# Delta rule preparation: the deferred projection matmuls of a tile in one gap at its end in place of three gaps inside it

## The chip, the cores and the metric

One Trainium2 chip (trn2), one of its cores. The metric is the device time of one execution in microseconds (us); each kernel's time is the median of its runs. Engines are named as in the profile: PE is TensorE (PEld its weight loads), DVE VectorE, ACT ScalarE, POOL GpSimd, SP SyncE, which here only issues DMAs.

## What is computed

The reference is a network of three layers in float32: an attention and gated-scan layer, a second gated-scan layer, and a layer that mixes pooling, a state-space scan and a gated delta rule, followed by experts. Only the delta rule's preparation matters here. For each chunk of 64 tokens and each of 6 heads (in both directions of time) it needs, of the normalised q and k:

```python
gc = jnp.cumsum(to_chunks(g), axis=-1)
decay = jnp.exp(jnp.where(lower, gc[..., :, None] - gc[..., None, :], -jnp.inf))
kb = kc * bc[..., None]
xm = jnp.where(strict, jnp.einsum('bnhik,bnhjk->bnhij', kb, kc) * decay, 0.0)
attn = jnp.einsum('bnhik,bnhjk->bnhij', qc, kc) * decay
```

Independent of it, the same layer needs the projection of the layer's input `hT` (1024 channels by 1024 tokens) onto 896 channels `xbcT`, which a later stage (a convolution) reads. The kernel computes this projection beside the delta rule's preparation.

## The kernel before, in words

The kernel is a sequence of stages; each is a function that writes the instruction stream of every engine by hand, with semaphores between them, and ends with a barrier of all engines. The stage here is `gdn_prepare` (line 2719). Its tile loop runs over ten tiles of 128 tokens (two chunks) in the order 8, 9, 0, 7, 1, 6, 2, 5, 3, 4 (`TILE_ORDER`); tiles 8 and 9 are context and have no attention product. The loop stands once in each engine's block, with `k` the place in the order. `GH` is 6 heads, in `PAIRS` = 3 pairs.

- PE (lines 2814 to 2841): `decays(k, 1)`, six matmuls of 128 columns into the two banks `ps_r`; transposes of q and k into `ps_t` (line 2824); `decays(k, 0)`, six matmuls into the same two banks (line 2808), which first waits for `arg_done`, that DVE has read the banks; the kk products (line 2832) and from the third tile on the kq products (line 2839).
- DVE (lines 2896 to 2903): `args(k, 1)` reads `ps_r` into `dec` (line 2875); `attend(k - 1)` (lines 2888, 2892); `norm(k + 2)` (line 2862); `args(k, 0)` (line 2877), which reads `ps_r` again.
- ACT (lines 2914 to 2928): moves q and k transposed to SBUF (line 2918), the kk products (line 2925), and takes the exponential of `dec` (line 2928) once `args(k, 0)` is done.
- POOL (lines 2790 to 2796): `H` = kk x decay (line 2793), then `attend(k - 1)` (line 2788).
- SP (lines 2755 to 2766): per tile four small DMAs of `H`'s diagonal blocks (line 2761) and, for the eight tiles with attention, two DMAs of 384 KB (line 2766).

The projection is the class `Background` (line 243). Its work is cut into units (7 here, of 128 channels, with one weight load of 512 KB each) and fills (14 here, two of 512 tokens per unit). A fill is 8 matmuls of 512 columns into one of two PSUM banks (line 342; in float32 each shows as two records), one move of the bank by ACT into one of three stage buffers (line 359) and one store of 256 KB by SP (line 304). The first `LEAD` = 3 fills run ahead of the loop. The matmuls of the others, 88, are dealt out evenly over the `slots` that the constructor is told:

```python
g = f if f < lead else lead + min(slots - 1, spent * slots // total)
```

A slot may hold parts of two fills. `multiply(pe, g)` (line 329) issues the matmuls of slot `g`; `move(act, g)` (line 351) moves the banks whose fill ended in slot `g - 1`; `transfer(sp, g)` (line 314) stores the fills that ended in slot `g - 2`, and loads the weights of the unit three further once a unit ended in slot `g - 1`. Ahead of a new fill PE waits for its bank's last move; ahead of a move ACT waits for the landing of the store that used its stage buffer before. Before the change a tile has three slots: behind `decays(k, 1)`, behind `decays(k, 0)`, and at the end of the tile (lines 2817, 2827, 2841). The next stage, `gdn_base`, begins with memsets on POOL (line 2977).

Of the kernel before, what the change touches and what calls it, by code (L numbers as in the profile page):

```python
# [21 lines left out]
def wait(eng, sem, value):  # L22

    if not isinstance(value, int) or value > 0:
        eng.wait_ge(sem, value)


def own_semaphores(nc, ctx, tag):

    used = []  # L30

    def clear():
        nc.clear_and_free_semaphores(used)
        nc.all_engine_barrier()

    def make(name):
        used.append(nc.alloc_semaphore(name=f"{tag}_{name}"))
        return used[-1]

    ctx.callback(clear)  # L40
    return make
# [2185 lines left out]
T2 = ROWS2 // P  # L2227
# [487 lines left out]
def unit_of(t, d):  # L2715
    return next(2 * s + d for s in range(STEPS) if order(s, d) == t)


def gdn_prepare(nc, tag, tok, beta, cum, logs, k_n, qT, kT, H, beta_rows, diag, attn_out, jobs):

    LEAD = 3
    with ExitStack() as ctx:
        sb = lambda n, s, d=F32: ctx.enter_context(nc.sbuf_tensor(f"{tag}_{n}", s, d))
        sem = own_semaphores(nc, ctx, tag)
        pbank = lambda n: ctx.enter_context(nc.psum_tensor(f"{tag}_{n}", [P, BANK], F32))
# [14 lines left out]
         arg_done, kk_moved, exp_done, kq_done, h_done, beta_turned, beta_moved, beta_stored, diag_stored) = (sem(n) for n in names)  # L2740
        att_done = [sem(f"att_done{d}") for d in range(2)]
        att_stored = [[sem(f"att_stored{d}{b}") for b in range(2)] for d in range(2)]
        bg = Background(sb, sem, pbank, jobs, 3 * T2, 3, 2, 3, lead=LEAD)
        block = ctx.enter_context(nc.Block())

        @block.sync
        def _(sp):
            for n, dst in ((1, k_n), (0, q_n)):
                sp.dma_start(dst[:, :, :], tok[:, n * GW:(n + 1) * GW].rearrange("(t p) c -> p t c", p=P)).then_inc(loaded, 16)
            bg.begin(sp)  # L2750
            sp.wait_ge(beta_moved, 1)
            sp.dma_start(beta_rows, beta_T[0:2 * T2 * GH, :]).then_inc(beta_stored, 16)
            for g in range(LEAD):
                bg.transfer(sp, g)
            for k, t in enumerate(TILE_ORDER):
                for n in range(3):
                    bg.transfer(sp, LEAD + 3 * k + n)
                b, at = k // HALF, k % HALF * GH
                sp.wait_ge(h_done, k + 1)
                for q in range(QUARTERS):  # L2760
                    sp.dma_start(diag[b, q, at:at + GH, :].rearrange("h (j i) -> j h i", i=SUB),
                                 H[SUB * q:SUB * (q + 1), t, :, SUB * q:SUB * (q + 1)]).then_inc(diag_stored, 16)
                if t < TILES:
                    for d in range(2):
                        sp.wait_ge(att_done[d], k - CTX_STEPS + 1)
                        sp.dma_start(attn_out[unit_of(t, d)], att[d][:, k % 2, :, :].rearrange("p h i -> p (h i)")).then_inc(att_stored[d][k % 2], 16)
            bg.end(sp)
            sp.wait_ge(beta_stored, 16)
            sp.wait_ge(diag_stored, 16 * QUARTERS * T2)
            for d in range(2):  # L2770
                for b in range(2):
                    sp.wait_ge(att_stored[d][b], 16 * TILES // 2)
# [25 lines left out]
        @block.tensor  # L2798
        def _(pe):
            pe.wait_ge(consts, 1)  # L2800
            pe.transpose(ps_t[0][0:2 * T2 * GH, 0:P], nbeta[:, :, :, :].rearrange("p k h d -> p (k h d)"), ident[:, :]).then_inc(beta_turned, 1)

            def decays(k, d):
                t = TILE_ORDER[k]
                wait(pe, arg_done, 2 * k + 1 - d)
                for h in range(GH):
                    col = 2 * SH + d * GH + h
                    last = pe.matmul(ps_r[h // 3][:, (h % 3) * P:(h % 3 + 1) * P], logs[:, t, col:col + 1].to_broadcast([P, P]),
                                     mask[:, d, :], start=True, stop=True)
                last.then_inc(r_made, 1)  # L2810

            for g in range(LEAD):
                bg.multiply(pe, g)
            for k, t in enumerate(TILE_ORDER):
                cols = slice(t * P, (t + 1) * P)
                decays(k, 1)
                bg.multiply(pe, LEAD + 3 * k)
                pe.wait_ge(normed, 2 * k + 2)
                if k == 0:
                    pe.wait_ge(beta_moved, 1)  # L2820
                for m, src in enumerate((q_n, k_n)):
                    wait(pe, kk_moved, 2 * k + m - 1)
                    for g in range(PAIRS):
                        last = pe.transpose(ps_t[m][:, g * P:(g + 1) * P], src[:, t, g * P:(g + 1) * P], ident[:, :])
                    last.then_inc(turned, 1)
                decays(k, 0)
                bg.multiply(pe, LEAD + 3 * k + 1)
                pe.wait_ge(t_moved, 2 * k + 2)
                for h in range(GH):
                    part = slice(GE * (h % 2), GE * (h % 2) + GE)  # L2830
                    out = slice(h // 2 * P, (h // 2 + 1) * P)
                    last = pe.matmul(ps_t[h % 2][:, out], kT[part, h // 2, cols], kT[part, h // 2, cols], start=True, stop=True)
                last.then_inc(kk_made, 1)
                if k >= CTX_STEPS:
                    wait(pe, kq_done, k - CTX_STEPS)
                    for h in range(GH):
                        part = slice(GE * (h % 2), GE * (h % 2) + GE)
                        out = slice(h // 2 * P, (h // 2 + 1) * P)
                        last = pe.matmul(ps_kq[h % 2][:, out], kT[part, h // 2, cols], qT[part, h // 2, cols], start=True, stop=True)
                    last.then_inc(kq_made, 1)  # L2840
                bg.multiply(pe, LEAD + 3 * k + 2)

        @block.vector
        def _(dve):
# [60 lines left out]
        @block.scalar  # L2905
        def _(act):
            act.wait_ge(beta_turned, 1)
            act.activation(beta_T[0:2 * T2 * GH, :], ps_t[0][0:2 * T2 * GH, 0:P], ACT.Copy).then_inc(beta_moved, 1)
            act.wait_ge(squared, 2 * T2)
            act.wait_ge(consts, 1)  # L2910
            act.activation(std[:, :, :], norms[:, :, :], ACT.Sqrt, bias=eps[:, 0:1]).then_inc(std_done, 1)
            for g in range(LEAD):
                bg.move(act, g)
            for k, t in enumerate(TILE_ORDER):
                bg.move(act, LEAD + 3 * k)
                for m, dst in enumerate((qT, kT)):
                    act.wait_ge(turned, 2 * k + m + 1)
                    act.activation(dst[:, :, t * P:(t + 1) * P], ps_t[m][:, 0:PAIRS * P].rearrange("p (g i) -> p g i", g=PAIRS),
                                   ACT.Copy).then_inc(t_moved, 1)
                bg.move(act, LEAD + 3 * k + 1)  # L2920
                act.wait_ge(kk_made, k + 1)
                wait(act, h_done, k - 1)
                for m in range(2):
                    out = kk[:, k % 2, :, :].rearrange("p (g m) i -> p m g i", m=2)[:, m]
                    act.activation(out, ps_t[m][:, 0:PAIRS * P].rearrange("p (g i) -> p g i", g=PAIRS), ACT.Copy).then_inc(kk_moved, 1)
                bg.move(act, LEAD + 3 * k + 2)
                act.wait_ge(arg_done, 2 * k + 2)
                act.activation(dec[:, k % 2, :, :], dec[:, k % 2, :, :], ACT.Exp).then_inc(exp_done, 1)
            bg.move(act, LEAD + 3 * T2)


def gdn_base(nc, tag, beta_rows, diag, lower_rows, upper_rows, jobs):
# [1228 lines left out]
```

## Time and profile before

| | us |
|---|---|
| median of 3 runs | 4562.99 |
| lowest, highest | 4560.31, 4571.77 |
| profiled execution, its own time | 4572.53 |
| span of the profiled execution, first to last instruction | 4570.8 |
| mean granted TensorE clock (share of full speed) | 0.902 |

The profile is of one execution. The page gives shares of the whole span; the stage of the change takes some 180 us of it, so it is read from the table of stretches (busy time of each engine between two times), the list of waits and the timeline, each for that stretch. Times in the timeline are from the span's start. Durations of matmuls are modelled and overlap the next one's; the distance from one start to the next is what PE takes.

### The profile page before, as it was taken

The numbers are of one execution on the slowest core, as the hardware profiler recorded it, in microseconds if no ns is written. First come the engines' busy times: TensorE is split into PE (matmuls) and PEld (weight loads), VectorE is DVE, ScalarE is ACT, GpSimd is POOL, SyncE is SP. The second block draws the span as 40 slices with busy tenths as digits, with TensorE's granted clock in tenths as the row PEclk, the third lists the DMA queues.
The fourth block names the chain that finished last, engine by engine and source line by source line (L and its number), as shares of the span: only waits on it lengthen the run. The fifth ranks groups of instructions, "written<-read, shape, count | busy, mean of one in ns | idle before, by whom it ended". The sixth has DMA issues, their size and how long they took to land. (4 is left out here: it accounts for less than half of the span.)

```text
span 4570.8 us, 48008 instructions
## 1 busy us (share of the span) xinstructions
PE 3763.4 (82%) x17093; PEld 2428.5 (53%) x17093; DVE 1523.2 (33%) x3680; ACT 1077.4 (24%) x2188; POOL 1013.3 (22%) x911
## 2 busy tenths in 40 slices
PE   7899998997989999999997938967755836765996
PEld 3545776763445666665684425654445835332442
DVE  1012223321532433535431220054476547142001
ACT  0023333321322333323323420021112101110111
POOL 0000002321331333333432440001302534110110
PEclk9999998998999999999998967988877858877998
DMA  3243213247421111111114321362334520444996
GB/s 103 75 124 92 80 40 106 86 147 244 153 97 38 45 50 54 38 47 41 56 43 190 124 101 56 91 165 84 108 83 124 175 92 24 172 165 144 318 318 225
DMA packets 423952, 516.34 MB, mean 113 GB/s; under 512 B 71954, under 2 KB 327482, under 8 KB 423731
## 3 DMA queue, kind: packets, MB, share of 16 engines
q1 hardware_dynamic: 390131, 473.04, 31.3%
q10 hardware_dynamic: 28992, 23.65, 1.6%
q0 software_dynamic: 4608, 16.78, 1.4%
q8 instruction: 130, 2.13, 0.2%
q14 instruction: 91, 0.75, 0.1%
HBM read 378.70 MB, written 134.68 MB: 112 GB/s over the span
## 5 line engine op out<-in xcount | busy, mean ns | idle before, releaser
L622 PE MATMUL hgrn_ps_w<-xT,hgrn_ring 128*128 128x512 f32 x1152 | 507.6, 596 | 0.0
L594 POOL TENSOR_TENSOR hgrn_queries<-hgrn_qd,hgrn_pair_decay 128x640 f32<-128x640 f32 x192 | 285.6, 1506 | 415.0 <-PE hgrn_ps_a L673 198.5
L622 PEld LDWEIGHTS hgrn_ps_w<-xT,hgrn_ring 128*128 128x128 f32 x1152 | 217.0, 192 | 251.7 <-issue 251.6
L1139 PE MATMUL end_ps_z<-end_w,end_yT 128*128 128x512 f32 x768 | 338.1, 600 | 4.4 <-ACT end_yT L1088 2.4
L618 PE MATMUL hgrn_ps_w<-hgrn_ring,xT 128*128 128x256 f32 x1536 | 337.8, 379 | 0.0
L618 PEld LDWEIGHTS hgrn_ps_w<-hgrn_ring,xT 128*128 128x128 f32 x1536 | 289.0, 190 | 38.2 <-issue 0.5
L1139 PEld LDWEIGHTS end_ps_z<-end_w,end_yT 128*128 128x128 f32 x768 | 146.6, 193 | 185.7 <-issue 178.7
L774 DVE COPY_PREDICATED hgrn_scores<-hgrn_mask,hgrn_ps_s 128x128 f32<-128x128 uint32 x192 | 48.5, 297 | 469.0 <-issue 466.7
L346 PE MATMUL gla_bg_ps<-gla_bg_w,xT 128*128 128x256 f32 x768 | 187.6, 397 | 4.6 <-DMA gla_bg_w<-in_w_in_ab_dram 4.6
L346 PEld LDWEIGHTS gla_bg_ps<-gla_bg_w,xT 128*128 128x128 f32 x768 | 150.6, 200 | 38.0 <-issue 10.8
L872 ACT ACTIVATE hgrn_k_tok<-hgrn_ps_a 128x256 f32<-128x256 f32 x84 | 32.3, 384 | 548.8 <-PE hgrn_ps_a L648 548.8
L240 DVE COPY in_stage<-in_ps 128x512 f32<-128x512 f32 (+4 forms) x29 | 17.8, 615 | 394.8 <-PE in_ps L184 303.2
L342 PE MATMUL att_bg_ps<-xT,att_bg_w 128*128 128x512 f32 (+1 forms) x288 | 135.5, 610 | 13.1 <-POOL att_ident L1442 13.1
L184 PE MATMUL in_ps<-hT_cols,in_wbuf 128*128 128x512 f32 x288 | 126.6, 603 | 0.0
L1516 DVE COPY att_stage<-att_ps_o 128x128 f32<-128x128 f32 x96 | 28.0, 292 | 291.7 <-PE att_ps_o L1478 291.7
L1703 POOL TENSOR_TENSOR gla_queries<-gla_qd,gla_pair_decay 128x640 f32<-128x640 f32 x64 | 84.2, 1334 | 184.3 <-PE gla_ps_o L1766 130.6
L1537 ACT ACTIVATE att_p_sb<-att_s_sb,att_shift 128x256 f32<-128x256 f32 (+1 forms) x192 | 88.8, 464 | 146.9 <-DVE att_shift L1512 146.9
L184 PE MATMUL in_ps<-xT,in_wbuf 128*128 128x512 f32 x256 | 112.6, 603 | 13.0 <-DMA in_wbuf<-in_w_in_ab_dram 13.0
L3990 PE MATMUL exp_ps_d<-expw_wd,exp_hidT 128*128 128x512 f32 x256 | 114.1, 599 | 11.0 <-ACT exp_hidT L3937 11.0
L346 PE MATMUL att_bg_ps<-att_bg_w,xT 128*128 128x256 f32 x512 | 122.5, 385 | 0.0
L342 PE MATMUL gdnp_bg_ps<-hT,gdnp_bg_w 128*128 128x512 f32 x224 | 106.5, 617 | 18.4 <-DMA gdnp_bg_w<-in_w_in_dram 9.5
L579 POOL TENSOR_TENSOR hgrn_kd<-hgrn_key,hgrn_rel 128x1024 f32<-128x1024 f32 x24 | 59.9, 2497 | 277.3 <-ACT hgrn_rel L861 277.1
(575 smaller groups left out, 6743.6 us busy)
## 6 DMA issues: line engine op xcount, KB each, us to landing
expw_wg<-in_exp_w_gate_dram SPq DMA_DIRECT2D x16, 2048.0 KB, 10.6
expw_wu<-in_exp_w_up_dram SPq DMA_DIRECT2D x16, 2048.0 KB, 16.2
expw_wd<-in_exp_w_down_dram SPq DMA_DIRECT2D x16, 2048.0 KB, 21.8
gla_bg_w<-in_ada_w_dram SPq DMA_DIRECT2D x24, 1024.0 KB, 5.3
hgrn_ring<-in_w_in_c_dram SPq DMA_DIRECT2D x36, 512.0 KB, 4.0
end_gt<-gate_l SPq DMA_DIRECT2D x16, 768.0 KB, 7.2
hgrn_ring<-in_w_in_c_dram SPq DMA_DIRECT2D x12, 1024.0 KB, 5.4
hgrn_o<-hgrn_o_stage SPq DMA_DIRECT2D x192, 64.0 KB, 2.6
```

The lines of the kernel that those rows point to most:

```text
L184: last = pe.matmul(bank[0:job.rows, 0:job.span], w[:, k, b * job.rows:(b + 1) * job.rows], job.acts[:, k, s:s + job.span], start=(k == 0), ...
L342: last = pe.matmul(bank[0:job.rows, 0:job.span], w[:, k, b * job.rows:(b + 1) * job.rows], job.acts[:, k, s:s + job.span], start=(k == 0), ...
L346: last = pe.matmul(bank[0:job.rows, q * job.width:(q + 1) * job.width], job.acts[:, k, t * P:t * P + job.rows], w[:, k, 0:job.width], star ...
L579: pool.tensor_tensor(kd[:, b, d, :], key[:, d, :], rel[:, d, :], ALU.mult).then_inc(k_done, 1)
L594: pool.tensor_tensor(queries[:, d, s, :].rearrange("p (b a c) -> p b a c", b=POINTS, a=PC), q, f, ALU.mult).then_inc(queries_done, 1)
L618: last = pe.matmul(bank[:, q * 2 * P:(q + 1) * 2 * P], xT[:, k, t * P:(t + 1) * P], wt[:, k, :], start=(k == 0), stop=(k == KB - 1))
L622: last = pe.matmul(bank[:, :], wt[:, k, 0:P], xT[:, k, part * BANK:(part + 1) * BANK], start=(k == 0), stop=(k == KB - 1))
L774: dve.copy_predicated(scores[:, d, p % 2, :], mask[:, d, :].bitcast(U32), ps_s[g % 2][:, d * P:(d + 1) * P]).then_inc(scores_done, 1)
L1139: made = pe.matmul(ps_z[h][:, :], yT[:, k, :], w[:, k, h * BANK:(h + 1) * BANK], start=(k == 0), stop=(k == NB - 1))
L1537: last = act.activation(p_sb[:, s % 2, h, 0:wide(d)], s_sb[:, s % 2, h, 0:wide(d)], ACT.Exp, bias=shift[:, s % 2, h:h + 1], scale=0.125, a ...
L1703: pool.tensor_tensor(queries[:, d, s, :].rearrange("p (b a c) -> p b a c", b=POINTS, a=PC), q, f, ALU.mult).then_inc(queries_done, 1)
L3990: last = pe.matmul(ps_d[g][:, :], hidT[:, j, :], wd[:, b, j, g * BANK:(g + 1) * BANK], start=(j == 0), stop=(j == FB - 1))
```

## The change

The constructor is told `T2` = 10 slots where it was told 30. On PE the calls of `multiply` behind the two decay groups go, and the one at the end of the tile stays. On ACT the moves ahead of kk and ahead of the exponential go, and the one at the top of the tile stays. On SP one `transfer` per tile stays of three. `LEAD`, the rings, banks and stage buffers stay as they are.

```diff
-        bg = Background(sb, sem, pbank, jobs, 3 * T2, 3, 2, 3, lead=LEAD)
+        bg = Background(sb, sem, pbank, jobs, T2, 3, 2, 3, lead=LEAD)
...
             for k, t in enumerate(TILE_ORDER):
-                for n in range(3):
-                    bg.transfer(sp, LEAD + 3 * k + n)
+                bg.transfer(sp, LEAD + k)
...
                 decays(k, 1)
-                bg.multiply(pe, LEAD + 3 * k)
                 pe.wait_ge(normed, 2 * k + 2)
...
                 decays(k, 0)
-                bg.multiply(pe, LEAD + 3 * k + 1)
                 pe.wait_ge(t_moved, 2 * k + 2)
...
-                bg.multiply(pe, LEAD + 3 * k + 2)
+                bg.multiply(pe, LEAD + k)
...
             for k, t in enumerate(TILE_ORDER):
-                bg.move(act, LEAD + 3 * k)
+                bg.move(act, LEAD + k)
...
-                bg.move(act, LEAD + 3 * k + 1)
                 act.wait_ge(kk_made, k + 1)
...
-                bg.move(act, LEAD + 3 * k + 2)
                 act.wait_ge(arg_done, 2 * k + 2)
...
-            bg.move(act, LEAD + 3 * T2)
+            bg.move(act, LEAD + T2)
```

## Rows read from the trace of the kernel before

**Rows 1.** The page: busy time of the engines, us (share of span) and instructions

```profile
PE 3763.4 (82%) x17093; PEld 2428.5 (53%) x17093; DVE 1523.2 (33%) x3680; ACT 1077.4 (24%) x2188; POOL 1013.3 (22%) x911
```

**Rows 2.** Stretch: its us, busy us (count) PE PEld DVE ACT POOL, clock, DMA share, GB/s

```profile
3145.50:3258.50 113.00, 113.00 (x623) 70.66 (x622) 48.39 (x142) 28.66 (x56) 24.82 (x14) 1.00 0.26 81
```

**Rows 3.** Waits from 3143 to 3275 us: total us, times, longest

```profile
DVE gdnp_dec L2875 <- PE gdnp_ps_r L2808: 64.2, 10, 7.6
```

**Rows 4.** Timeline of a steady tile (k = 5): start us, us, engine, line

```profile
3207.34 1.50 PE L2808 MATMUL gdnp_ps_r<-gdnp_mask,logs 128*128 128x128 f32 x12
...
3208.67 2.74 PE L342 MATMUL gdnp_bg_ps<-hT,gdnp_bg_w 128*128 128x512 f32 x6
...
3208.94 1.64 DVE L2875 TENSOR_SCALAR gdnp_dec<-gdnp_ps_r,cum 128x128 f32<-128x128 f32 x6 [5.64 <-PE gdnp_ps_r L2808]
...
3210.50 1.01 DVE L2888 TENSOR_TENSOR gdnp_kq<-gdnp_ps_kq,gdnp_dec 128x384 f32<-128x384 f32 x2
...
3211.25 0.49 PE L2824 MATMUL gdnp_ps_t<-gdnp_ident,gdnp_q_n 128*128 128x128 f32 x3
...
3211.91 1.50 PE L2808 MATMUL gdnp_ps_r<-gdnp_mask,logs 128*128 128x128 f32 x12
3212.16 0.48 ACT L2918 ACTIVATE gdn_kT<-gdnp_ps_t 128x384 f32<-128x384 f32 x1
...
3213.24 2.74 PE L342 MATMUL gdnp_bg_ps<-hT,gdnp_bg_w 128*128 128x512 f32 x6
...
3213.59 1.65 DVE L2877 SCALAR_TENSOR_TENSOR gdnp_dec<-gdnp_ps_r,cum,gdnp_dec 128x128 f32<-128x128 f32 x6
...
3215.92 0.94 PE L2832 MATMUL gdnp_ps_t<-gdn_kT 64*128 64x128 f32 x12
...
3216.90 0.87 ACT L2925 ACTIVATE gdnp_kk<-gdnp_ps_t 128x384 f32<-128x384 f32 x2 [4.25 <-PE gdnp_ps_t L2832]
...
3217.45 2.84 PE L342 MATMUL gdnp_bg_ps<-hT,gdnp_bg_w 128*128 128x512 f32 x6
3217.66 0.60 ACT L359 ACTIVATE gdnp_bg_stage<-gdnp_bg_ps 128x512 f32<-128x512 f32 x1
...
3218.14 0.85 ACT L2928 ACTIVATE gdnp_dec<-gdnp_dec 128x768 f32<-128x768 f32 x1
...
3220.13 1.50 PE L2808 MATMUL gdnp_ps_r<-gdnp_mask,logs 128*128 128x128 f32 x12
```

**Rows 5.** Timeline of the second scan stage: PE starts on a release by DVE

```profile
1470.94 0.49 DVE L763 TENSOR_TENSOR hgrn_k_end<-hgrn_kd,hgrn_end_decay 128x128 f32<-128x128 f32 x2
1471.49 0.20 PEld L648 LDWEIGHTS hgrn_ps_a<-hgrn_ident,hgrn_k_end 128*128 128x128 f32 x2 [0.57 <-DVE hgrn_k_end L763]
```

**Rows 6.** Timeline of the stage's tail, from the last tile's first decay group

```profile
3258.53 1.50 PE L2808 MATMUL gdnp_ps_r<-gdnp_mask,logs 128*128 128x128 f32 x12
...
3263.78 10.64 SPq L2766 DMA_DIRECT2D gdn_attn<-gdnp_att  x2
...
3268.85 0.84 ACT L2928 ACTIVATE gdnp_dec<-gdnp_dec 128x768 f32<-128x768 f32 x1
...
3271.54 4.28 POOL L2788 TENSOR_TENSOR gdnp_att<-gdnp_kq,gdnp_mask 128x768 f32<-128x768 f32 x2
...
3274.95 2.17 SPq L2761 DMA_DIRECT2D gdnp_diag<-gdn_H  x4
...
3278.12 0.47 SPq L304 DMA_DIRECT2D xbcT<-gdnp_bg_stage  x1
3282.35 0.21 POOL L2977 MEMSET gdnb_rows<- 128x128 f32 x1 [6.53 <-POOLq L34]
```

**Rows 7.** DMA issues from 3140 to 3300 us: count, KB each, us to landing

```profile
xbcT<-gdnp_bg_stage SPq DMA_DIRECT2D x12, 256.0 KB, 2.8
```

**Rows 8.** Stretches behind an idle time of PE, and with short ones (columns as rows 2)

```profile
3137.00:3141.00 4.00, 4.00 (x6) 1.79 (x7) 2.42 (x6) 0.29 (x1) 0.00 (x0) 0.59 0.76 191
...
950.00:960.00 10.00, 6.67 (x47) 5.57 (x46) 7.56 (x15) 1.47 (x3) 3.72 (x2) 1.00 0.33 116
```

## The prediction, made before the changed kernel was run

> **What bounds the kernel now.** I read the page first: TensorE (PE) is busy for 82% of the span, no other engine for more than 53% even with PE's own weight loads counted [rows 1]. The page's chain of waits is followed back only a short way, through the last stage, and says nothing of this one, so I went to that stage, `gdn_prepare`, with the table of stretches: its tile loop runs from 3145.5 us, and tiles 0 to 8 fill 113.0 us in which PE is busy all 113.0 and the granted clock is 1.00, the upper of its two levels, 2.4 GHz [rows 2]. The list of waits in the loop has DVE, ACT and POOL waiting for PE or for each other, the largest for PE being DVE's 64.2 us on the first decay group [rows 3], and no wait of PE. The loop is bound by PE's own instructions.
>
> The timeline of one steady tile (k = 5) is what the working rests on [rows 4]. PE's starts give the pitch of each part: first decay group 3207.34 to 3208.67, 1.33 us; three deferred matmuls (each shows as two records) to 3211.25, 2.58; six transposes to 3211.91, 0.66; second decay group to 3213.24, 1.33; three deferred to 3215.92, 2.68; kk and kq, twelve records each, to 3217.45, 1.53, so about 0.77 each; three deferred to 3220.13, 2.68. Sum 12.79 us, with nothing between. One deferred matmul costs 0.86 (2.58/3); the other two gaps are 0.10 longer, and I take that for the switch to the narrower matmuls behind them.
>
> **The change, part by part.** The 88 deferred matmuls behind the lead were spread over 30 gaps of three (two of them have two: the third of tile 4 and the very last); by the same rule of `Background` they now fall into 10 gaps of 9, 9, 9, 9, 8, 9, 9, 9, 9, 8. Nothing is computed more or less.
>
> (a) PE's work. The nine deferred matmuls of a tile cost the same in one place. Two of three switches to wide matmuls and back go. The one at the transposes shows no price, the one at the next tile's decay group stays, and the one at kk saves between 0 and 0.10, according to whether kk behind other 128-column matmuls costs the same bubble. I take 0.07 off.
>
> (b) The gap between the decay groups was cover. The second group, `decays(k, 0)`, overwrites the two banks that DVE is still reading for the first, so it waits for `arg_done`. DVE begins 1.60 us after the first group's start (3208.94) and needs six instructions, 1.64 us [rows 4], so it is done at 3.24. Today PE comes to that wait at 3211.91 - 3207.34 = 4.57 and never stops. Without the gap it comes at 1.33 + 0.66 = 1.99. How soon PE starts after DVE is shown by the scan stage: DVE ends at 1470.94 + 0.49 = 1471.43, PE's weight load starts at 1471.49 [rows 5], 0.06 later; I add 0.05 for a weight load that no running matmul hides. The group starts at 3.35: **a new stall of 1.36 us per tile**, in all ten. Bounds: 1.25 (no wake-up) and 1.42 (0.06, and a whole pitch of a decay record, 1.33/12 = 0.11, unhidden).
>
> (c) The gap before kk covered ACT's moves of qT and kT. It is not missed: the transposes are out at about 2.2, ACT's two moves of 0.48 end near 3.0, and the second decay group ends only at 3.35 + 1.33 = 4.68. kq needs DVE's first half of attend(k-1): 3.24 + 1.01 = 4.3, against kq's start at 5.5 [rows 4]. Cost nothing; if this cover went, kk would wait for ACT.
>
> (d) The other chain. DVE's second arguments start where they do now, since DVE has attend and norm in between: 3213.59 - 3207.34 = 6.25, end 7.9. But today ACT's Exp starts only at 3218.14, 10.8 into the tile, because kk and a bank's move stand ahead of it. Now kk ends near 5.7, ACT's copies (0.87) near 6.6, Exp runs 7.9 to 8.8, and POOL's `H` and attend(k-1), 2.1 each by the pair in [rows 6], end by 13. This is off PE's path, PE being at its nine deferred matmuls from 6.3 to 14.0. Nothing in it becomes later.
>
> (e) Moves, stores and loads. At the top of a tile ACT moves at most what the last gap filled, 0.60 us each [rows 4], before the transposes are out at 2; once, in tile 9, two banks, the second held until fill 9's store has landed (issued near 12.9 of tile 8, 2.8 later landed), so ending near 2.2 and then delaying qT by 0.3, still ahead of 4.68. SP's stores come two gaps after the fill, which is now two tiles in place of two thirds of one; three stage buffers just carry that. Weight loads are issued from tiles 1, 3 and 5 for use in 4, 6 and 8: tens of us ahead. Cost nothing inside the loop.
>
> Tile length: 12.79 + 1.36 - 0.07 = 14.08, that is +1.29 (1.25 - 0.10 = 1.15 to 1.42). The last tile starts nine tiles in: **+11.6 us** (10.4 to 12.8).
>
> (f) The tail. From the last tile's start, 3258.53, Exp ends at 3269.69, 11.16 in; POOL runs H and the two last attends; SP is behind it: it is held by tile 8's att (issue ends at 3263.78 + 10.64 = 3274.42), then issues a store, four diag (2.17), two att (about 1.0, from 3277.1 to 3278.12) and the last store (0.47) to 3278.59, and with 2.8 us to landing the stage ends near 3281.4, 22.9 in [rows 6, 7]. In the changed tile Exp ends at about 7.85, 3.3 earlier. The chain behind it moves with it: SP's last att issue ends at 16.25. Against that, fills 11 and 12 are now stored there too, two issues more, 2 x 0.48; last issue at 17.7, landing 20.5. PE's last eight matmuls, 6.9 us from 6.3, end at 13.2 and the last bank moves by 16.2 even if it waits for the store of fill 10 to land; that is hidden behind SP. Three stores and two att close together share the queues: I give back 0.4. So **-2.0 us**, between -3.3 (Exp's whole lead) and +1.9 (lead worth nothing, 0.96 of issues and as much again of traffic).
>
> Sum: 11.6 - 2.0 = **+9.6 us**. Against the profiled execution's own 4572.53 (span 4570.8) that is 4582.1; that execution lies 9.5 us above the median of the three runs, 4562.99, and nothing in it is particular to this stage, so I put the sum on the median: **4572.6 us**, +0.21%. What a measurement of this kernel can tell from no change is about 0.3%, 13.7 us, so this counts as no change.
>
> **Rivals.** *The clock falls.* Waits come back into a loop that had none. After PE's long idle time before the third lead bank the clock is 0.59 over four us, 4 x 0.41 = 1.64 us of full-speed work lost [rows 8]; in each of nine tiles that is +14.8, in all +24.4, 4587 us, slower. It decides as soon as three tiles in nine do it (9.6 + 3 x 1.64 = 14.5). Against it: a stretch of ten us in another stage has PE busy for 6.67 us only and still a granted clock of 1.00 [rows 8], and here PE would be busy for 12.7 in 14.1. The Trainium skill (TensorE: Matmul & The Clock Gate, "A second HAM failure mode: psum-queue depth-cycling") tells of a kernel whose short idle times between groups of matmuls made the clock go back and forth; by that rule each of the ten waits could cost a slow start. The trace so far does not agree. Chance 0.05.
>
> *The tail takes instead of giving.* The mechanism is the ring of three stage buffers: the last bank may be moved only when fill 10's store has landed, and this store stands on SP behind POOL's attend(8); then three stores follow the att pair. At +1.9 in place of -2.0, with a stall of 1.42, the sum is 12.8 + 1.9 = +14.7, 4577.7, slower. It decides if the tail gives nothing back and a tile grows by 1.5. For it: SP is the last engine at work already [rows 6]. Against: Exp's lead of 3.3 us is plain arithmetic. With the scatter of the runs (11 us over three) that can push a true +9.6 over the line: 0.20.
>
> *Faster.* That needs the removed switches to be worth more than the stall: rows allow 0.10 a tile at the most against 1.25, unless the tail or the scatter gives it. To end at -13.7 some 23 us would have to come from nowhere. That the change does not do what it says (PE would not stop at the second group, since DVE had finished there) is ruled out by the order of the code unless DVE's work is shorter than its record. Both together 0.05.
>
> **The numbers.** Forecast 0.70. Its own range is 10.4 - 3.3 = +7.1 to 12.8 + 1.9 = +14.7, and 3 to 4 us on either side for the scatter of medians: 4566 to 4581. This holds the forecast and the tail rival; the clock's 4587 is left out. Faster 0.05, same 0.70, slower 0.25.
>
> **What would show it.** In the changed profile: starts of the first decay group 14.0 to 14.1 us apart; a wait of PE at the second decay group on DVE's first arguments, ten times, 1.2 to 1.4 us; no wait of PE at kk; granted clock 1.00 throughout the loop; Exp near 8 us into the tile; from the last tile's start to the next stage's first POOL memset about 22 us where it is 23.8 now [rows 6]. I would be wrong if the tile grew by more than 1.5, if PE waited at kk for ACT, or if a clock below 1.00 stood in the loop.

## The result, and the profile after

The changed kernel took 4577.34 us (median of 8 runs, 4570.51 to 4590.55), the kernel before 4570.01 (median of 8, 4560.31 to 4574.23; the three runs shown above are among them). The ratio is 1.0021 with a 95% interval of 1.0012 to 1.0031, which is +9.6 us (5.5 to 14.2) on 4570: a small loss, inside the 0.3% that the prediction called no change, but clear of zero. (The two medians differ by 7.3 us, which lies in the same interval.)

The profiled execution of the changed kernel has a span of 4574.6 us, only 3.8 more than the one before; it reached the first tile 5.9 us sooner (3139.60 against 3145.54), so the two are compared stage by stage and not by their spans. Line numbers of the stage have moved up by one to five (the decay groups are now L2807, the first arguments L2872). The page first:

```profile
PE 3760.2 (82%) x17093; PEld 2425.0 (53%) x17093; DVE 1519.9 (33%) x3680; ACT 1078.9 (24%) x2188; POOL 1011.6 (22%) x911
```

The same 17093 matmul records, the same shares [rows 1]: nothing of the change is to be seen here. The stretch of tiles 0 to 8, in the table of stretches (length, then busy time and count of PE, PEld, DVE, ACT and POOL, then clock, DMA share and GB/s):

```profile
3139.60:3265.20 125.60, 115.27 (x623) 72.73 (x622) 48.39 (x142) 30.29 (x56) 26.84 (x15) 1.00 0.24 74
```

It had been 113.0 us with PE busy throughout [rows 2]; now it is 125.6, with the same 623 PE records, DVE's busy time to the hundredth what it was, and some 10 us in which PE does nothing. The granted clock is still 1.00. The list of waits in the stage (total us, times, longest) says who waits:

```profile
DVE gdnp_dec L2872 <- PE gdnp_ps_r L2807: 81.1, 10, 9.2
...
ACT gdnp_bg_stage L359 <- DMA xbcT<-gdnp_bg_stage: 14.0, 2, 7.6
...
PE gdnp_ps_r L2807 <- DVE gdnp_dec L2872: 11.5, 10, 1.2
...
ACT gdnp_dec L2923 <- DVE gdnp_dec L2874: 6.8, 7, 1.2
```

Third line: a wait of PE that the kernel before did not have, ten times, 1.15 us each, at the second decay group, on DVE's first arguments. No line has PE waiting at kk. ACT's two waits for the landing of a store are new too; neither holds up another engine (the first ends before the transposes are out, the second before SP comes to that bank's store). In the timeline a tile is read from one first decay group to the next. A steady tile, k = 6 in the timeline:

```profile
3222.63 1.50 PE L2807 MATMUL gdnp_ps_r<-gdnp_mask,logs 128*128 128x128 f32 x12
...
3223.86 0.36 PEld L2822 LDWEIGHTS gdnp_ps_t<-gdnp_ident,gdnp_q_n 128*128 128x128 f32 x3
3223.97 0.49 PE L2822 MATMUL gdnp_ps_t<-gdnp_ident,gdnp_q_n 128*128 128x128 f32 x3
...
3224.24 1.65 DVE L2872 TENSOR_SCALAR gdnp_dec<-gdnp_ps_r,cum 128x128 f32<-128x128 f32 x6 [7.91 <-PE gdnp_ps_r L2807]
...
3225.93 1.41 PEld L2807 LDWEIGHTS gdnp_ps_r<-gdnp_mask,logs 128*128 128x128 f32 x12 [1.39 <-DVE gdnp_dec L2872]
3225.94 1.60 PE L2807 MATMUL gdnp_ps_r<-gdnp_mask,logs 128*128 128x128 f32 x12 [1.15 <-DVE gdnp_dec L2872]
...
3227.47 0.75 PEld L2829 LDWEIGHTS gdnp_ps_t<-gdn_kT 64*128 64x128 f32 x12
3227.47 0.94 PE L2829 MATMUL gdnp_ps_t<-gdn_kT 64*128 64x128 f32 x12
...
3228.13 0.75 PEld L2836 LDWEIGHTS gdnp_ps_kq<-gdn_qT,gdn_kT 64*128 64x128 f32 x12
3228.24 0.84 PE L2836 MATMUL gdnp_ps_kq<-gdn_qT,gdn_kT 64*128 64x128 f32 x12
...
3229.01 0.30 PEld L342 LDWEIGHTS gdnp_bg_ps<-hT,gdnp_bg_w 128*128 128x128 f32 x2
3229.01 7.99 PE L342 MATMUL gdnp_bg_ps<-hT,gdnp_bg_w 128*128 128x512 f32 x18
...
3230.57 0.84 ACT L2923 ACTIVATE gdnp_dec<-gdnp_dec 128x768 f32<-128x768 f32 x1 [1.24 <-DVE gdnp_dec L2874]
...
3236.84 1.50 PE L2807 MATMUL gdnp_ps_r<-gdnp_mask,logs 128*128 128x128 f32 x12
```

The tile is 14.21 us long against 12.79 [rows 4]. The second decay group starts 3.31 us in, right behind DVE's 1.61 + 1.65; it reached this point at 4.57 before, and had it been free to go it would have started at 2.0. (The profile's 1.15 counts from the modelled end of the transposes; by starts the group is 1.31 late.) Exp starts 7.9 into the tile where it was 10.8. And the tail, from the last tile's first decay group to the next stage's first POOL memset:

```profile
3265.25 1.50 PE L2807 MATMUL gdnp_ps_r<-gdnp_mask,logs 128*128 128x128 f32 x12
...
3272.26 0.84 ACT L2923 ACTIVATE gdnp_dec<-gdnp_dec 128x768 f32<-128x768 f32 x1 [0.30 <-DVE gdnp_dec L2874]
...
3274.95 4.29 POOL L2787 TENSOR_TENSOR gdnp_att<-gdnp_kq,gdnp_mask 128x768 f32<-128x768 f32 x2
3277.88 0.43 SPq L304 DMA_DIRECT2D xbcT<-gdnp_bg_stage  x1
3278.36 2.17 SPq L2760 DMA_DIRECT2D gdnp_diag<-gdn_H  x4
3280.57 0.91 SPq L2765 DMA_DIRECT2D gdn_attn<-gdnp_att  x2
3280.69 0.60 ACT L359 ACTIVATE gdnp_bg_stage<-gdnp_bg_ps 128x512 f32<-128x512 f32 x1 [7.59 <-DMA xbcT<-gdnp_bg_stage]
3281.53 2.15 SPq L304 DMA_DIRECT2D xbcT<-gdnp_bg_stage  x3
3287.14 0.21 POOL L2972 MEMSET gdnb_rows<- 128x128 f32 x1 [7.90 <-POOLq L34]
```

3265.25 to 3287.14 is 21.89 us; it was 23.82 [rows 6]. Exp, ACT's exponential of `dec`, starts 7.01 into the last tile and not 10.32. So the stage gained 1.93 us at its end and lost 125.65 - 112.99 = 12.66 in nine tiles: +10.7 us, as much as the runs show within their interval. Two readings are used below for every kernel: the **loop** (nine tiles, first decay group of tile 0 to that of tile 9; before 112.99) and the **tail** (from there to the memset; before 23.82). "The att pair" is SP's two issues of 384 KB for the last tile; three stores of 256 KB follow it here, where one did before.

The busy share of the core's DMA engines at the end of the tail, in tenths, 40 slices a row; in the kernel before from 3274 to 3285 us, in the changed one from 3277 to 3288 with the GB/s of each slice:

```profile
DMA  0006999998941529999999996000000000000000
```

```profile
DMA  0000299999994523699999999999999100000000
GB/s 0 0 0 0 78 391 380 402 335 402 343 176 62 83 38 52 257 380 391 380 447 369 402 346 402 387 358 402 395 365 387 52 0 0 0 0 0 0 0 0
```

From the att pair on the DMA engines work without a pause, 2.7 us for 1.05 MB before and 4.2 us for 1.57 MB after, and the memset follows some 1.5 us behind their end in both. The last store is issued by 3283.68 and its traffic ends only near 3285.6: here the bytes set the end, at some 390 GB/s, and each further store of 256 KB takes 0.67 us of it (an estimate from that rate).

### The profile page after: what moved, and what is told of

Same layout as the page of the kernel before. It is cut to its first block and busy times, and to the rows that moved or that the text cites. A ratio compares the mean times of both kernels' runs of the same rounds, so it can differ in the third digit from the quotient of the medians.

```text
span 4574.6 us, 48008 instructions
## 1 busy us (share of the span) xinstructions
PE 3760.2 (82%) x17093; PEld 2425.0 (53%) x17093; DVE 1519.9 (33%) x3680; ACT 1078.9 (24%) x2188; POOL 1011.6 (22%) x911
## 5 line engine op out<-in xcount | busy, mean ns | idle before, releaser
L342 PE MATMUL att_bg_ps<-xT,att_bg_w 128*128 128x512 f32 (+1 forms) x288 | 135.1, 609 | 13.1 <-POOL att_ident L1442 13.1
L184 PE MATMUL in_ps<-xT,in_wbuf 128*128 128x512 f32 x256 | 112.0, 600 | 12.8 <-DMA in_wbuf<-in_w_in_ab_dram 12.8
```

The costliest lines, as they stand in the source:

```text
L184: last = pe.matmul(bank[0:job.rows, 0:job.span], w[:, k, b * job.rows:(b + 1) * job.rows], job.acts[:, k, s:s + job.span], start=(k == 0), ...
L342: last = pe.matmul(bank[0:job.rows, 0:job.span], w[:, k, b * job.rows:(b + 1) * job.rows], job.acts[:, k, s:s + job.span], start=(k == 0), ...
```

## The experiments

The theory: the gap between the two decay groups covered DVE's first arguments; without it PE waits once per tile, and only this costs. The rival: one long gap in itself costs, by its switches, its bank waits or its late moves and stores, and the place of the gap matters little. For the tail: the chain Exp, then POOL's `H` and attend, then SP's issues one by one sets the end; its rival is that the last bank of the projection does (PE's matmuls, ACT's move, SP's store). Each kernel was timed beside the kernel before on the same chip.

**How much cover is needed.** e1 and e2 take after and put two, or one, of a tile's nine deferred matmuls back behind the first decay group. `multiply` is given a first and a last place within the slot; moves and stores stay as in after. The edit of e1; e2 has 1 where it has 2:

```diff
                 decays(k, 1)
+                bg.multiply(pe, LEAD + k, 0, 2)
                 pe.wait_ge(normed, 2 * k + 2)
...
-                bg.multiply(pe, LEAD + k)
+                bg.multiply(pe, LEAD + k, 2)
```

> As after, but the first two of a tile's nine deferred matmuls stand behind the first decay group, the other seven at the end of the tile. Cover theory (the lost time is DVE's 1.64 us on the first arguments, uncovered): PE comes to the second decay group at 1.34 + 1.72 + 0.66 = 3.7 us, later than DVE's end at 3.24, so no wait of PE on DVE; tile 12.8 to 12.9 us (after: 14.21, before: 12.79); the last tile to the next stage's memset stays at about 21.9 (before: 23.8); in all about 2 us less than before and 12 less than after's stage. Rival (the single long gap itself costs: switches, bank waits, late moves and stores): the tile stays at 13.5 or more, since seven of nine still stand in one gap.

> As after, but one of the nine deferred matmuls stands behind the first decay group. Cover theory: PE comes to the second group at 1.34 + 0.86 + 0.66 = 2.86, PE is held some 0.3 to 0.45 us in each of ten tiles; tile 13.3 to 13.4; stage about 3 us over before. Rival: 13.5 or more, no clear step between one and two matmuls.

Measured: e1 loop 112.97, tile 12.80, tail 21.87, no wait of PE; 0.9992 of the kernel before (0.9983 to 1.0001). e2 loop 117.93, tile 13.35, tail 21.89; 1.0002 (0.9993 to 1.0011). The waits of PE at the second decay group in e2:

```profile
PE gdnp_ps_r L2812 <- DVE gdnp_dec L2878: 2.9, 10, 0.3
```

Zero, one and two matmuls of cover give waits of 1.15, 0.29 and 0 us and tiles of 14.21, 13.35 and 12.80. The first step is 0.86, one matmul; the second is only 0.55, what was left to cover. Seven of nine in one gap cost nothing; whether nine do is settled by e6. The first of e1's tail rows also settles a term of my sum:

```profile
3258.07 1.50 PE L2812 MATMUL gdnp_ps_r<-gdnp_mask,logs 128*128 128x128 f32 x12
...
3259.50 0.94 PE L2835 MATMUL gdnp_ps_t<-gdn_kT 64*128 64x128 f32 x12
```

kk starts 1.43 behind the decay group's start, not 1.33: kk has a bubble (a short idle time of PE) of 0.10 behind narrow matmuls as well.

**Which of the gaps.** e3 and e4 have two gaps of four or five matmuls per tile. e3 leaves out only the one ahead of kk; e4 leaves out only the one between the decay groups. The edit of e3 against the kernel before; in e4 the call behind `decays(k, 1)` goes and the one behind `decays(k, 0)` stays. ACT's moves and SP's transfers follow the two slots.

```diff
-        bg = Background(sb, sem, pbank, jobs, 3 * T2, 3, 2, 3, lead=LEAD)
+        bg = Background(sb, sem, pbank, jobs, 2 * T2, 3, 2, 3, lead=LEAD)
...
                 decays(k, 1)
-                bg.multiply(pe, LEAD + 3 * k)
+                bg.multiply(pe, LEAD + 2 * k)
...
                 decays(k, 0)
-                bg.multiply(pe, LEAD + 3 * k + 1)
...
-                bg.multiply(pe, LEAD + 3 * k + 2)
+                bg.multiply(pe, LEAD + 2 * k + 1)
```

> Two gaps per tile, behind the first decay group and at the end, 4 or 5 matmuls each; the gap ahead of kk alone is gone. Cover theory: no wait of PE, tile 12.7 to 12.8, Exp of the last tile some 1.3 us earlier than before, tail about 22.5; 1 to 2 us less than before. Rival (kk and ACT's moves needed the gap ahead of kk): PE waits at kk and the tile is 13.3 or more.

> Two gaps per tile, behind the second decay group and at the end; the gap between the decay groups alone is gone. Cover theory: PE held at the second decay group by 1.15 us in all ten tiles as after, tile 14.2, and since kk comes late again the tail is not shortened: about 23.8; stage 12.7 us over before, that is 2 more than after. Rival (the number of gaps matters, not the place): half of after's loss, tile 13.5, as e3.

Measured: e3 loop 112.96, tail 22.91; 0.9995 (0.9986 to 1.0004). e4 loop 125.68, tail 24.21; 1.0026 (1.0017 to 1.0035). e4's waits:

```profile
ACT gdnp_kk L2923 <- PE gdnp_ps_t L2831: 68.7, 10, 7.4
...
PE gdnp_ps_r L2808 <- DVE gdnp_dec L2874: 11.5, 10, 1.2
```

The same 11.5 us of PE as in after, with two gaps per tile: the place decides, not the number. And as kk comes late again, ACT waits for it and Exp starts 10.02 into the last tile; the tail's gain is gone. Both tails are 0.4 longer than expected (e3 22.91 against 22.5, with Exp at 8.71; e4 24.21 against 23.8): SP issues two stores behind tile 8's att where it issued one before, 0.94 and 0.95 us against 0.43.

**Take the wait away with the gap left out.** e5 and e6 leave all nine matmuls at the tile's end and make the hand-over finer. In e5 DVE reports after three heads (one bank) and after six; in e6 PE does too, and DVE waits for each half. The edit of e6; e5 leaves the lines with `r_made` as they were. In both, ACT's wait ahead of Exp becomes `4 * k + 4`:

```diff
-                wait(pe, arg_done, 2 * k + 1 - d)
                 for h in range(GH):
+                    if h % 3 == 0:
+                        wait(pe, arg_done, 4 * k + 2 * (1 - d) - 1 + h // 3)
...
-                last.then_inc(r_made, 1)
+                    if h % 3 == 2:
+                        last.then_inc(r_made, 1)
...
-                dve.wait_ge(r_made, 2 * k + 2 - d)
+                    if h % 3 == 0:
+                        dve.wait_ge(r_made, 4 * k + 2 * (1 - d) + 1 + h // 3)
...
-                last.then_inc(arg_done, 1)
+                    if h % 3 == 2:
+                        last.then_inc(arg_done, 1)
```

> As after, but DVE reports the first arguments after three heads and again after six, and PE's second decay group waits for its three heads at a time. The deferred matmuls stay in their one gap. Cover theory: the first three heads are free at 1.60 + 0.82 = 2.4, the second three at 3.24 to 3.31; the second group ends 0.65 to 0.75 earlier than in after, tile 13.5 to 13.6. Rival (the single gap costs by itself): no change against 14.21.

> As e5, and PE also reports the decay groups after three heads, so that DVE begins half a group earlier. Cover theory: DVE is done at about 2.6 and the first half at 1.8, before PE needs them at 2.0 and 2.66; no wait of PE, tile 12.8 to 12.9 with all nine deferred matmuls in one gap, and Exp some 0.6 us earlier, so the tail is 21.2 to 21.9; 2 to 3 us less than before. Rival: 13.5 or more.

Measured: e5 loop 119.62, tile 13.54, tail 21.89; 1.0003 (0.9992 to 1.0013); PE still waits ten times, 0.37 us each. e6 loop 113.00, tile 12.80, tail 21.15; 0.9993 (0.9983 to 1.0003). e6's timeline, the tile that begins at 3219.44:

```profile
3219.44 1.50 PE L2808 MATMUL gdnp_ps_r<-gdnp_mask,logs 128*128 128x128 f32 x12
3220.31 1.65 DVE L2875 TENSOR_SCALAR gdnp_dec<-gdnp_ps_r,cum 128x128 f32<-128x128 f32 x6 [6.14 <-PE gdnp_ps_r L2808]
...
3221.43 1.51 PE L2808 MATMUL gdnp_ps_r<-gdnp_mask,logs 128*128 128x128 f32 x12
...
3222.87 0.94 PE L2831 MATMUL gdnp_ps_t<-gdn_kT 64*128 64x128 f32 x12
...
3224.41 7.99 PE L342 MATMUL gdnp_bg_ps<-hT,gdnp_bg_w 128*128 128x512 f32 x18
```

DVE starts 0.87 into the tile and not 1.61, and PE goes on at 1.99 without a stop, with one long gap as in the changed kernel. This is the strictest test: the change keeps its shape, all nine matmuls in one gap, and its whole loss in the loop, 12.65 us, is gone with the wait.

**The tail.** e7 is e1, and e8 is e6, with 13 of the 88 matmuls in the last tile (8 before), the other 75 spread over nine tiles.

```diff
-                g = f if f < lead else lead + min(slots - 1, spent * slots // total)
+                even = 0 if f < lead else spent * slots // total if not at_end else spent * (slots - 1) // (total - at_end * self.columns(f))
+                g = f if f < lead else lead + min(slots - 1, even)
...
+        bg = Background(sb, sem, pbank, jobs, T2, 3, 2, 3, lead=LEAD, at_end=13)
```

> e1 with 13 of the 88 deferred matmuls in the last tile in place of 8, the other 75 spread over nine tiles. Tail theory (the end of the stage is set by the chain Exp, POOL, SP, beside which PE is free from 13 on): the last tile starts 5 x 0.86 = 4.3 us earlier against e1 and the tail stays at 21.9 to 22.5, so about 6 us less than before. Rival (the last bank's move and store set the end): the tail grows by what the start gains, and nothing is won.

> e6 with the same 13 matmuls in the last tile. By both theories together 6 to 7 us less than before; by the rival of the tail 2 to 3.

Measured: e7 loop 108.67, tail 21.88; 0.9990 (0.9980 to 1.0000). e8 loop 108.70, tail 21.15; 0.9987 (0.9977 to 0.9997). Five matmuls leave the nine tiles, 4.3 us, and the tail does not grow by 0.1 us: PE's work at the end of the last tile is hidden behind the chain. The rival's bound, the last bank, is not reached.

e9 is after, and e10 is e8, with the stores that can go early issued ahead of SP's wait for tile 8's att.

```diff
-                bg.transfer(sp, LEAD + k)
+                if k < T2 - 1:
+                    bg.transfer(sp, LEAD + k)
...
+                if k == T2 - 2:
+                    bg.transfer(sp, LEAD + T2 - 1)
+                    bg.transfer(sp, LEAD + T2)
                 if t < TILES:
```

(`end` leaves out what was so done.)

> As after, but SP issues the stores of fills 10, 11 and 12 ahead of its wait for tile 8's att in place of behind it. Chain theory (from Exp of the last tile the stage's end hangs on POOL's attend(8) and the DMAs that SP then issues one by one): 0.48 for fill 10 and 0.69 for each of the others leave the chain, so last tile to memset 21.89 - 1.86 = 20.0; loop 125.6 unchanged; stage about 189.2. Rival (PE's last eight matmuls, ACT's last move or the landing of the att DMAs set the end): the tail stays above 21.5.

> e8 with fill 10's and fill 11's stores ahead of the wait. By the chain alone the tail would be 21.15 - 1.17 = 20.0. But with 13 matmuls in the last tile PE ends at 16.4 of it, the bank is moved at 17.0 and its store issued by 17.5, and 3.5 more to the memset is 21.0: so 20.9 to 21.1, the last bank now being the bound. Loop 108.7. In all 7 us less than before.

Measured: e9 loop 125.65, tail 19.80; 1.0020 (1.0010 to 1.0029). e10 loop 108.70, tail 20.13; 0.9979 (0.9969 to 0.9988). e9's tail:

```profile
3265.45 1.50 PE L2811 MATMUL gdnp_ps_r<-gdnp_mask,logs 128*128 128x128 f32 x12
3265.83 1.41 SPq L304 DMA_DIRECT2D xbcT<-gdnp_bg_stage  x3
...
3280.06 0.91 SPq L2769 DMA_DIRECT2D gdn_attn<-gdnp_att  x2
3281.01 0.48 SPq L304 DMA_DIRECT2D xbcT<-gdnp_bg_stage  x1
3285.25 0.21 POOL L2976 MEMSET gdnb_rows<- 128x128 f32 x1 [5.83 <-POOLq L34]
```

Three issues leave the chain and 2.09 us leave the tail (1.86 expected). They leave it in two parts. Ahead of the att pair it is SP's issues: with fill 10's store gone the pair starts 14.61 into the tile and not 15.32, 0.71 sooner. Behind the pair 1.38 us go with two stores, and there the DMA engines had worked without a pause, which points to their bytes (1.34 us by the rate above) rather than to the time SP takes to issue them; no run separates the two, since moving a store moves both. e10's tail was expected at 20.9 to 21.1, bound by the last bank:

```profile
3250.64 1.50 PE L2813 MATMUL gdnp_ps_r<-gdnp_mask,logs 128*128 128x128 f32 x12
...
3265.47 2.54 SPq L305 DMA_DIRECT2D xbcT<-gdnp_bg_stage  x2
3267.07 0.60 ACT L360 ACTIVATE gdnp_bg_stage<-gdnp_bg_ps 128x512 f32<-128x512 f32 x1 [6.27 <-PE gdnp_bg_ps L343]
3270.77 0.21 POOL L2981 MEMSET gdnb_rows<- 128x128 f32 x1 [6.89 <-POOLq L34]
```

The last bank is indeed moved behind the att pair, at 16.4 to 17.0 as expected, and SP waits for it; but the memset comes only 2.76 us behind the last issue (3268.01), against 3.46 in after and 3.76 before. The DMA engines from 3262 to 3272 us show why:

```profile
DMA  0002999993605299999998995089800000000000
```

They have finished the pair and the store ahead, and stand idle in one slice (3268.25 to 3268.5), before the last store's traffic begins; in after they still had 1.9 us of work when the last store had been issued. The memset is again 1.5 us behind the end of the traffic.

All in one table (us; sum is loop and tail together against the 136.81 of before; the last column is the ratio times 4570, less 4570):

| kernel | loop | tail | Exp in last tile | sum against before | runs |
|---|---|---|---|---|---|
| before | 112.99 | 23.82 | 10.32 | | |
| after | 125.65 | 21.89 | 7.01 | +10.7 | +9.6 |
| e1 | 112.97 | 21.87 | 7.00 | -2.0 | -3.7 |
| e2 | 117.93 | 21.89 | 7.00 | +3.0 | +0.9 |
| e3 | 112.96 | 22.91 | 8.71 | -0.9 | -2.3 |
| e4 | 125.68 | 24.21 | 10.02 | +13.1 | +11.9 |
| e5 | 119.62 | 21.89 | 7.00 | +4.7 | +1.4 |
| e6 | 113.00 | 21.15 | 6.26 | -2.7 | -3.2 |
| e7 | 108.67 | 21.88 | 7.00 | -6.3 | -4.6 |
| e8 | 108.70 | 21.15 | 6.26 | -7.0 | -5.9 |
| e9 | 125.65 | 19.80 | 7.00 | +8.6 | +9.1 |
| e10 | 108.70 | 20.13 | 6.25 | -8.0 | -9.6 |

The runs follow the stage to within their intervals, some 4 us either way. Nothing outside the stage has to be called on. e10 beats the kernel before, 4556.73 us against 4565.35 in the same comparison, with an interval that ends at 0.9988; beside the changed kernel, itself above the one before, it was not timed. e1, e3 and e6 can't be told from the kernel before by their runs.

## Why the prediction was right

- **The bound.** PE's own instructions bound the loop. e1, e3 and e6 move the deferred matmuls in three ways, and each brings the loop back to 113.0.
- **(a) PE's work.** I took 0.07 us a tile off for a switch saved at kk. It is 0.00, and the reading behind it was wrong: the 0.10 is not the price of going from wide matmuls to narrow ones. It stands at kk's start behind a decay group too (e1), and the other one stands at the start of the gap behind kq, not at its end: of the gaps in [rows 4] this one's record lasts 2.84 us and the others' 2.74. Both are where PE changes between weights of 128 rows and of 64, and in the steady tile above the first weight load there begins together with its matmul (3227.47, 3229.01), while at the transposes it begins 0.11 ahead (3223.86). A tile goes into the 64-row work and out of it once in either kernel, so nothing could be saved. That the row count is the cause was not tested by itself.
- **(b) The stall.** Predicted start of the second group 3.35 into the tile, measured 3.31; but the first of its records is held by 0.10 (1.60 us for the group in place of 1.50, and 1.53 to kk in place of 1.43). So 1.31 later and 0.10 slower, 1.42 in all, where I had 1.36: my upper bound, nearly the whole pitch (0.11) of a weight load that no running matmul hides, as the trace has it (load at 3225.93, matmul at 3225.94). With (a) the tile grew by 1.42, not 1.29, and the loop by 12.7, not 11.6; the range given reached to 12.8.
- **(c) and (e).** PE never waits at kk or for a bank in the loop. ACT's second move in the last tile was held by fill 9's landing, as forecast, and ended 1.1 into the tile where I had 2.2, since fill 9's store had been issued at 11.9 of tile 8 and not 12.9.
- **(d) and (f).** Exp at 7.9 in a steady tile, 7.01 in the last, as worked out. The tail gave 1.93 against 2.0 expected. The lead of 3.31 us reached the end of the att pair whole (16.23 into the tile against my 16.25). What the two further stores cost, 1.38, I had as 0.96 of issues and 0.4 given back for shared queues: the size is right, but the rows above put nearly all of it on the traffic. The three last stores took 2.15 to issue, not 1.4, and the end came 3.46 behind the last issue, not 3.76.
- **The sum.** +9.6 predicted; +10.7 in the stage by the two profiles; +9.6 (5.5 to 14.2) by the runs. That the last agrees to the digit is luck: the loop was mis-sized by 1.1 us, and the interval is 9 us wide. The time, 4577.3, is 4.7 above the 4572.6 of the forecast because the kernel before itself came out 7.0 higher over eight runs than over the three that I had; the medians lie 7.3 apart and not 9.6.
- **The rivals.** The clock did not fall: the granted clock was 1.00 (the upper level, 2.4 GHz) over all nine tiles with a wait of 1.15 us in each. The Trainium skill's case of a clock that goes back and forth with short idle times (TensorE: Matmul & The Clock Gate, "A second HAM failure mode: psum-queue depth-cycling") was not met at waits of this length and spacing. The tail's rival put the last bank behind a full ring: the move did wait for fill 10's landing, ending 16.0 into the tile, but SP came to its store only later.

## What to carry to other kernels

Work that fills a gap on the bounding engine is judged by what the gap covers: look for the semaphore behind it, and for how much later its release comes than PE would; here that was 1.3 us, covered by two matmuls of nine but not by one, and the rest could stand in one gap at the end. The same wait could be removed without any cover by handing over one bank at a time instead of two. And where a stage ends in a chain on other engines, give the bounding engine more of its deferred work in that tail (five matmuls there were worth 4.3 us) and issue ahead of the last wait the stores that are ready, so that neither their issues nor their bytes stand at the end.

## What I had not expected

- Going into kk's 64-row weights costs PE 0.10 us whatever stands before: 1.43 from a decay group's start in e1 and 1.44 in e6, against 1.33 into other 128-row work. Going back out of them costs as much (a gap's record of 2.84 us against 2.74, [rows 4]).
- Three 256 KB stores in a row behind the att pair take SP 2.15 us to issue (0.72 each), and three ahead of the wait in e9 take 1.41 (0.47 each). Most stores that are issued alone take 0.43 to 0.48, but one in the loop of the changed kernel (at 3235.47) took 1.57. What makes an issue long was not looked for.
- POOL's last two attends take 4.29 us together where a single one takes 1.81. The rows of each, in both kernels, put the excess on one of them, 2.5 us, which overlaps DVE's own attend, itself 1.56 in place of 0.96. That is a coincidence in the traces, not tested.
